# Three inner norms cut into two token halves, interleaved with the matmul units before and behind them

## What is computed

```python
h = modulate(rmsnorm(x, p['norm_mix_g']), mod[0], mod[1])
q, k, v, u_r, u_f = split_projection(h, p['w_in'])
...                                    # attention, RWKV scans, Fourier mixing -> o
x = x + g1 * o                         # o is the output projection
h = modulate(rmsnorm(x, p['norm_ffn_g']), sh2, sc2)
gt, up = jnp.split(h @ p['ffn_w_in'], 2, axis=-1)
return x + g2 * ((jax.nn.silu(gt) * up) @ p['ffn_w_out'])

def rmsnorm(x, g):
    y = x * lax.rsqrt(jnp.mean(x * x, axis=-1, keepdims=True) + RMS_EPS)
    return y * g
def modulate(h, shift, scale):
    return h * (1.0 + scale) + shift
```

## Time and profile before

| | |
|---|---|
| median of three runs | 1829.46 us (1827.52 to 1830.53) |
| span of the profiled execution | 1825.5 us |
| the profiled execution's own time | not given apart from its span; the median lies 3.96 us above the span |
| mean granted clock of TensorE | 0.996 |
| PE busy | 1741.5 us, 95% |
| DVE, ACT, POOL busy | 1064.4, 803.0 and 370.7 us |

### The profile page before, as it was taken

How to read it: one execution, slowest core, us unless ns; L and a number is a source line. 1 busy time by engine, 2 the same in 40 slices (tenths; PEclk the granted TensorE clock), 3 DMA queues, 4 the chain that set the end, 5 groups by cost and what they waited for, 6 DMA issues and landing times. The chain is left out here.

```text
span 1825.5 us, 46192 instructions
## 1 busy us (share of the span) xinstructions
PE 1741.5 (95%) x19693; PEld 1629.2 (89%) x19693; DVE 1064.4 (58%) x2330; ACT 803.0 (44%) x1729; POOL 370.7 (20%) x306
## 2 busy tenths in 40 slices
PE   7999988889999999999999999898999999999997
PEld 5999776779899999999989987777898999999997
DVE  4545777663494673838453566676519647365663
ACT  3343655542453351535443356464326525344352
POOL 3254010212202003020324431002231120201112
PEclk9999999999999999999999999999999999999999
DMA  9654401004513313141327360010122132323211
GB/s 338 211 131 145 120 5 49 6 4 135 168 59 89 85 60 103 58 115 53 99 83 202 97 193 21 17 36 7 29 66 56 63 108 64 105 61 90 84 56 58
DMA packets 215973, 161.11 MB, mean 88 GB/s; under 512 B 21968, under 2 KB 213146, under 8 KB 215770
## 3 DMA queue, kind: packets, MB, share of 16 engines
q1 hardware_dynamic: 213818, 156.13, 29.0%
q0 software_dynamic: 1952, 2.03, 0.4%
HBM read 154.99 MB, written 3.15 MB: 87 GB/s over the span
## 5 line engine op out<-in xcount | busy, mean ns | idle before, releaser
L2683 DVE SCALAR_TENSOR_TENSOR x<-PS,mod,x 128x320 f32<-128x320 f32 (+2 forms) x240 | 90.8, 434 | 289.3 <-PE PS L1082 289.3
L1118 PE MATMUL PS<-T_hi,wsplit 128*128 128x320 f32 x768 | 170.0, 309 | 0.0
L822 POOL TENSOR_TENSOR SfR<-ring,SfR 128x768 fp32r<-128x768 f32 (+1 forms) x24 | 41.1, 1712 | 582.3 <-ACT SfR L1792 582.3
L1081 PE MATMUL PS<-in_hi,win 128*128 128x320 f32 x480 | 149.9, 320 | 0.7 <-POOL win L822 0.7
L1082 PE MATMUL PS<-in_hi,win 128*128 128x320 f32 x480 | 144.6, 309 | 0.0
L1081 PE MATMUL PS<-hid_hi,wsplit 128*128 128x320 f32 x440 | 133.0, 310 | 0.0
L1082 PE MATMUL PS<-hid_hi,wsplit 128*128 128x320 f32 x440 | 132.5, 309 | 0.0
L1118 PEld LDWEIGHTS PS<-T_hi,wsplit 128*128 128x128 f32 x768 | 128.4, 188 | 0.0
L1118 PE MATMUL PS<-h_hi,wsplit 128*128 128x320 f32 x576 | 127.6, 309 | 0.0
L1118 PE MATMUL PS<-T_lo,wsplit 128*128 128x320 f32 x384 | 118.7, 309 | 0.0
L2110 ACT ACTIVATE wsplit<-Sf 128x512 fp32r<-128x512 f32 x96 | 59.8, 629 | 130.0 <-DVE Sf L2733 72.3
(11 more groups left out here) (540 smaller groups left out, 5407.2 us busy)
## 6 DMA issues: line engine op xcount, KB each, us to landing
ring<-in_w_ada SPq DMA_DIRECT2D x47, 1024.0 KB, 6.7
ring<-in_ffn_w_in SPq DMA_DIRECT2D x88, 512.0 KB, 5.2
ring<-in_ffn_w_out SPq DMA_DIRECT2D x16, 768.0 KB, 4.3
ring<-in_ffn_w_out SPq DMA_DIRECT2D x16, 640.0 KB, 4.0
ring<-in_w_in SPq DMA_DIRECT2D x7, 1024.0 KB, 9.5
ring<-in_w_in SPq DMA_DIRECT2D x10, 512.0 KB, 6.0
ring<-in_w_in SPq DMA_DIRECT2D x16, 256.0 KB, 6.0
ring<-in_w_out SPq DMA_DIRECT2D x16, 256.0 KB, 5.8
```

The lines of the kernel that those rows point to most:

```text
L822: nc.gpsimd.tensor_tensor(lo, raw_w, hi, SUB).then_inc(wl_ready(), 1)
L1081: mm(lat[:, 0:TH], w, v[:, 0:TH], start=(n == 0), stop=(n == total - 1))
L1118: last = mm(bank[:, 0:TH], (w_lo if p == 1 else w_hi)[:, k, :], (v_lo if p == 2 else v_hi)[:, k, :], start=(q in (A11, A12, S1_) and k == ...
L2683: last = V.scalar_tensor_tensor(x[:, m, a:b], bank[:, at:at + b - a], mod[:, gate_at + m, s:s + 1], x[:, m, a:b], MUL, ADD)
```

## The change

The two units in front of each inner norm and the two behind it run by token halves, with the norm's steps in between.

- `last_two`: left half of unit 6, `pair_part` of tile 5, left half of unit 7, then (only at A) the modulation matmuls, then the right halves of both, into which the sums (`half_sums`) and the spread (`half_spread`) of the left half are put.
- `first_two`: for each half the products with the high parts of both units, tile by tile, then those with the residues. The sums of the right half stand behind tile 4 of the left half, its spread behind tile 7.
- Scaling on DVE is a plain product of `x` and the spread result (`half_scale`); gain and shift go together on ACT (`half_high`). For residues of tiles 0 to 3 ACT writes `h` in full precision (`half_full`) and POOL subtracts (`low_half`); for tiles 4 to 7 DVE does both (`half_low`).
- The first scale of the left half waits for the whole of unit 7 (`ready(names[1])`). The `warm` matmuls at the inner norms go. Weights of FFN0 and FFN0 + 1 get places of their own and are split earlier. The parameters of layer 1 are turned earlier; two entries leave the list of PSUM items.

```diff
+                def low_half(la, which, half):
+                    hi, lo = (h_hi, h_lo) if which else (in_hi, in_lo)
+                    c = slice(TH * half, TH * half + TH)
+                    for k in range(KP):
+                        e.wait_ge(full_act.sem, full_act.upto(la, KP * (2 * which + half) + k + 1))
+                        nc.gpsimd.tensor_tensor(lo[:, k, c], h[:, k, c], hi[:, k, c], SUB).then_inc(hl_pool(), 1)
...
-                for u in range(FFN0, NUNIT):
+                weight_low(FFN0)
+                weight_low(FFN0 + 1)
+                low_half(l, 1, 0)
+                weight_low(FFN0 + 2)
+                low_half(l, 1, 1)
+                for u in range(FFN0 + 3, NUNIT):
...
+                def half_sums(la, which, half):
+                    e.wait_ge(sq_ready.sem, sq_ready.upto(la, which * (KT + 2) + KT + 2 * half))
+                    for k in (KT - 2, KT - 1):
+                        for c in (2 * half, 2 * half + 1):
...
+                def half_spread(la, which, half):
+                    e.wait_ge(rms_inv.sem, rms_inv.upto(la, 2 * which + half + 1))
...
                 def first_two(u):
-                    on_high = [(k, p) for k in range(KT) for p in (0, 1)]
...
-                    unit(u, on_high, 3 * KT)
-                    unit(u + 1, on_high, 3 * KT)
-                    unit(u, on_low, 3 * KT, len(on_high))
-                    unit(u + 1, on_low, 3 * KT, len(on_high))
+                    for half in range(2):
+                        for k in range(KT):
+                            for v in (u, u + 1):
+                                unit(v, [(k, 0), (k, 1)], 3 * KT, 2 * k, (half,), half == 0)
+                            if half == 0 and k == KP:
+                                half_sums(l, which, 1)
...
+                            half_spread(l, which, 1)
+                        unit(u, on_low, 3 * KT, 2 * KT, (half,))
+                        unit(u + 1, on_low, 3 * KT, 2 * KT, (half,))
+
+                def last_two(u, order, total, cut, la, which, done, between):
+                    unit(u, order, total, 0, (0,)).then_inc(done, 1)
+                    pair_part(which, PAIR_ENDS[-1])
+                    unit(u + 1, order, total, 0, (0,)).then_inc(done, 1)
+                    between()
+                    unit(u, order[:10], total, 0, (1,))
+                    half_sums(la, which, 0)
+                    unit(u, order[10:], total, 10, (1,))
+                    unit(u + 1, order[:cut], total, 0, (1,))
+                    half_spread(la, which, 0)
+                    unit(u + 1, order[cut:], total, cut, (1,))
...
-                for m in range(2, KT):
+                for m in range(2, KT - 2):
...
-                pair_part(1, KT - 1)
-                warm(3)
-                inverse(1)
-                warm(4)
+                last_two(NPROJ + KT - 2, early + late, 3 * KT, 4, l, 1, left_out.sem, next_rows)
...
+                for k in range(KT):
+                    half_high(l, 1, 0, k)
+                    if k == 1:
+                        taken(e, l, ("out", KT - 1))
+                        half_square(l, 1, 1, KT - 1)
+                    if k == KP + 1:
+                        half_root(l, 1, 1)
+                half_full(l, 1, 0)
                 weight_high(FFN0 + 2)
+                act(root_table[:, :], eps[:, 0:1], ACT.Silu)
                 for k in range(KT):
...
+                    half_high(l, 1, 1, k)
+                half_full(l, 1, 1)
...
+            def half_low(l, which, half):
...
+                for k in range(KP, KT):
+                    e.wait_ge(h_ready.sem, h_ready.upto(l, KT * (2 * which + half) + k + 1))
+                    for s, a, b in HALVES[half]:
+                        last = V.tensor_scalar(h[:, k, a:b], h[:, k, a:b], gain[:, which, k, s:s + 1],
+                                               mod[:, 24 * which + k, s:s + 1], MUL, ADD)
+                    own.mark(last)
+                for k in range(KP, KT):
+                    e.wait_ge(dve_own, own.n - KT + 1 + k)
+                    V.tensor_tensor(lo[:, k, c], h[:, k, c], hi[:, k, c], SUB).then_inc(hl_ready(), 1)
...
+                    half_inverse(la, which, 0)
+                    free = [acc_free[ITEM_AT[name] % 2] for name in names]
+                    residual_half(names[0], KT - 2, gate_at, 1, None, 0).then_inc(free[0](), 1)
+                    ready(names[1])
+                    e.wait_ge(inv_ps.sem, inv_ps.upto(la, 2 * which + 1))
+                    half_scale(la, which, 0, 0)
+                    half_scale(la, which, 0, 1)
+                    residual_half(names[1], KT - 1, gate_at, 1, None, 0).then_inc(free[1](), 1)
+                    for k in range(2, KT):
+                        half_scale(la, which, 0, k)
+                    half_inverse(la, which, 1)
+                    half_low(la, which, 0)
```

More of the change, by code:

```diff
@@ L1001, in last_part @@
+                def half_spread(la, which, half):
+                    e.wait_ge(rms_inv.sem, rms_inv.upto(la, 2 * which + half + 1))
+                    r = slice(64 * half, 64 * half + 64)
+                    for i in range(2):
+                        last = mm(ps[6 + half][:, QW * i:QW * i + QW], mats[r, 5 + 2 * half + i, :], rot[r, 0:QW],
+                                  start=True, stop=True)
+                    last.then_inc(acc_ready() if which and half else inv_ps(), 1)
                 def last_part(k):
@@ L1052, in ada_cols, with unit @@
                     last.then_inc(mcol_ps(), 1)
-                def unit(u, order, total, first=0):
+                def unit(u, order, total, first=0, parts=(0, 1), held=False):
                     name, ck, g, nk = UNITS[u]
                     if first == 0:
-                        begin(name)
+                        if not held:
+                            begin(name)
                         e.wait_ge(wl_ready.sem, wl_ready.upto(l, u + 1))
@@ L1757, in _, with half_full @@
+            def half_full(l, which, half):
+                for k in range(KP):
+                    for s, a, b in HALVES[half]:
+                        last = act(h[:, k, a:b], h[:, k, a:b], ACT.Identity,
+                                   bias=mod[:, 24 * which + k, s:s + 1], scale=gain[:, which, k, s:s + 1])
+                    last.then_inc(full_act(), 1)
             for q_ in range(2):
                 e.wait_ge(xT_sb[q_], 5)
+            e.sem_inc(full_act(2 * KP), 2 * KP)
             for l in range(DEPTH):
@@ L2056, in _ @@
                     ada_rows(0, ahead)
-                for k in range(KT):
-                    if 0 < k and k + 2 < KT:
+                for k in range(KT - 2):
+                    if 0 < k:
                         weight_high(NPROJ + k + 2)
-                    elif k == KT - 1:
-                        weight_high(FFN0)
                     taken(e, l, ("out", k))
@@ new lines, in first_scale, with half_inverse @@
+                for k in tiles:
+                    e.wait_ge(h_ready.sem, h_ready.upto(0, 2 * (k + 1)))
+                    for s, (a, b) in enumerate(STREAMS):
+                        last = V.scalar_tensor_tensor(in_lo[:, k, a:b], h[:, k, a:b], mod[:, k, s:s + 1],
+                                                      in_hi[:, k, a:b], ADD, SUB)
+                    last.then_inc(hl_ready(), 1)
+            def half_inverse(l, which, half):
+                r = slice(64 * half, 64 * half + 64)
+                e.wait_ge(root_done.sem, root_done.upto(l, 2 * which + half + 1))
+                V.reciprocal(rot[r, 0:QW], rot[r, 0:QW]).then_inc(rms_inv(), 1)
@@ L2685, in residual, with residual_half @@
                     last.then_inc(free(), 1)
-                for m in range(KT):
+                def residual_half(name, m, gate_at, half, done, n):
+                    i, lat, cx = acc_item(name)
+                    if half:
+                        e.wait_ge(acc_ready.sem, acc_ready.upto(l, i + 1))
+                    else:
+                        e.wait_ge(done, n)
+                    for s, a, b in HALVES[half]:
+                        bank = (lat, cx)[half]
+                        last = V.scalar_tensor_tensor(x[:, m, a:b], bank[:, a - TH * half:b - TH * half],
+                                                      mod[:, gate_at + m, s:s + 1], x[:, m, a:b], MUL, ADD)
+                    return last
@@ new lines, in residual_norm @@
+                def residual_norm(la, which, names, gate_at, left, n0, left_done):
+                    for n, name in enumerate(names):
+                        residual_half(name, KT - 2 + n, gate_at, 0, left, n0 + n + 1).then_inc(left_done, 1)
+                    half_inverse(la, which, 0)
[10 more added lines that the diff above has]
+                    half_low(la, which, 0)
+                    if which:
+                        free, lat, cx = ready(("inv", 1))
+                    else:
+                        e.wait_ge(inv_ps.sem, inv_ps.upto(la, 2))
```

(13 more changed lines are left out.)

341 lines of the change are left out of this document (189 added, 152 removed).

## The result

The changed kernel takes **1860.1 us** (median of four runs, 1855.9 to 1863.1) against 1828.9 (four runs, 1827.5 to 1830.5): ratio 1.0165, 95% interval 1.015 to 1.018, so 1.7% slower. Forecast were 1844.5 us and a range of 1826 to 1852: the direction was right, the time lies above the range, and the loss is twice the 15 us of the sum. The profiled execution ran 1859.0 us, span 1857.1, mean granted clock 0.984 (before 1825.5 and 0.996).

A forecast was written before the change was run, and what follows sets the result against it. PE is busy 95% of the span, so a norm costs what PE loses around it. The three inner norms lose 6.1, 4.0 and 4.9 us, together 15.0, on 1829.5: 1844.5 us, range 1826 to 1852.

The forecast's parts named there:

- Front: Before the third inner norm PE waits from 3.5 to 5.9 us for POOL's squares; unit out 7 is whole at 18.5.
- Turns, left half: In the left residues behind a norm DVE and POOL alternate, one instruction each, so DVE ends at 14.95 us; chance 0.60.
- Rival 1: DVE and POOL do not hinder each other in the residues behind the norms: +2 us, 1831 in all; chance 0.18.
- Rival 2: PE never waits for a residue behind the norms: -14 us together, 1815 in all; chance 0.12.
- ACT does each tile in two pieces (192 and 128 columns), 0.65 a tile.: Right half behind the norm: ACT is slower than PE's 0.59 us a tile, last tile ready at 20.75 us.
- POOL's four turns alternate with DVE's: Right half's residues: POOL and DVE take turns after the rewritten `h`, POOL ending at 26.05 us.
- PEclk 1.00: Expected sign in the profile after: TensorE's clock stays at the 2.4 GHz level.
- rival 3: TensorE's clock falls without `warm` matmuls; right half's high products take 9.4 us, not 4.7, per norm: +29, 1859; chance 0.10.
- Ada chunks: At the first inner norm the modulation matmuls wait 1.4 us for their two 1 MB chunks, issued behind out 7's weight residue.
- At nothing: DVE's sums for the fast products behind the units cost nothing; 1 us at first and third inner norms if cover fails.

The follow-up runs named there:

- e2_early: Changed kernel with the weight split of unit FFN0 + 2 done before the left residues instead of behind them: 1857.4 us, ratio 1.0165.
- e4_dve: Changed kernel with the residues of all eight tiles on DVE in both halves, none on POOL: 1853.3 us, ratio 1.0141.
- e5_piece: Changed kernel with the right half's ACT and DVE scalar instructions in one piece of 320 columns, for timing only: 1851.5 us, ratio 1.0129.
- e1_warm: Changed kernel with matmuls that nobody reads put where PE waits behind the three inner norms: 1851.8 us, ratio 1.0143.
- e6_code: Changed kernel with 24 semaphore increments that nobody waits for in PE's program behind each of the first two inner norms: 1855.7 us, ratio 1.014.
- e10_ada: Changed kernel with the first inner norm's modulation matmuls moved from behind the left half of out 7 to behind its right half: 1857.4 us, ratio 1.0159.
- e11_place: Kernel before with only 24 semaphore increments that nobody waits for added in PE's program behind the first inner norm: 1834.5 us, ratio 1.0036.

## Why the prediction was right or wrong

Right, by its own steps:
- **Front.** PE waits 2.12 us in front of the third sum at C (2.3 forecast), 1.50 at B (1.7), none at A; E is 18.9 us behind the start at C (18.5) and 13.0 at B (12.4).
- **Turns, left half.** The first scale of the right half comes at E + 15.03 at C, E + 14.8 at A and E + 12.6 at B; the sum had 14.95 and, without the weight residue, 12.6. Rival 1 would have had DVE through at 9.7. e2_early and e4_dve show the turns by themselves. That the sum fits to 0.1 us at C is in part luck: DVE starts its part at E + 7.4 and not 6.9, its first two scalar instructions come 0.36 us apart and not 0.22, and the whole part lasts 7.6 us, not 8.0.
- **Rival 2** is out: the waits for residues at C are 0.46, 0.49, 0.66, 2.13, 1.27 and three of 0.41, together 6.2 us, over the 5.6 of its condition, though well under my 10.4.
- **Rival 1's price** has a slip at B: 34.5 against 34.6 is -0.1 and not +0.3. Nothing hangs on it.

Wrong, and the step that failed:
- **"ACT does each tile in two pieces (192 and 128 columns), 0.65 a tile."** It takes 0.84, and 0.85 for each rewritten `h` instead of 0.65. The last high product's tile is ready at E + 22.2 at C, 20.75 forecast; POOL's last residue is done at E + 27.7, 26.05 forecast. This is 1.5 us in each norm, and e5_piece shows that ACT's pace is what the right half waits for. I had interpolated between 512 and 128 columns, 0.71 and 0.39, of an instruction that adds the shift and nothing more. The changed instruction applies the gain too, as its scale, and that has a price of its own. The two forms on 128 columns, grouped by shape (busy us, mean ns), in the changed kernel at its first norm, which is not edited, and at C:

```profile
L1823 ACT ACTIVATE in_hi<-h,mod 128x128 fp32r<-128x128 f32 x8 | 3.1, 385 | 0.0
L1834 ACT ACTIVATE h_hi<-h,mod,gain 128x128 fp32r<-128x128 f32 x8 | 3.9, 481 | 0.0
```

That is 0.1 us an instruction, and 0.19 a tile of two pieces: the whole gap between 0.65 and 0.84. The change moved the gain from DVE to ACT, and the sum took this as free.
- **"POOL's four turns alternate with DVE's"** in the right half, with residues that PE takes 1.2 us apart. They do not: DVE does its four in a row, POOL's first is held for 2.09 us behind them, and PE takes POOL's residues 0.82 us apart. From POOL's first start to its last end it is 4.56 us, where 4.65 were forecast, so the sum does not show the fault; that is luck.
- **"PEclk 1.00", and rival 3 at 0.10.** The clock did fall, as the rival said, and its total of 1859 was met by accident. Its price was not: it put 4.7 us a norm on the right half's high products. They run under ACT's pace, and PE still waits 1.27 us (C) and 2.08 (A) for POOL's first residue behind them, so half clock is free there. Behind B it costs 1.7 us on the last 13 matmuls (e1_warm). Behind A and C these end together with DVE's held sum, so it costs nothing alone. In front of E it costs about 1.5 where it happens to stand (C in e1_warm, e2_early, e4_dve, e5_piece, e6_code and e10_ada). The Trainium skill (TensorE: Matmul & The Clock Gate, What's actually happening) says that an idle array drops to half clock; the trace agrees, with 0.88, 0.88 and 0.90 in the three windows where PE waits and no `warm` matmul stands.
- **Ada chunks.** 2.52 us instead of 1.4 at A; E comes 21.4 us behind the start, 19.9 forecast.
- **"At nothing": the fast products.** I had 1 us if the cover fails. DVE's first sum is held by POOL for 2.2 us more at A and C, and 1.3 us come back later.
- **Not in the sum at all:** 5.1 us in the recurrence of layer 1, which goes with the place of PE's code. The forecast looked only at the three norms and took every stretch that isn't edited as unchanged. e11_place loses as much there without the cut in halves, and e6_code takes the loss out of the changed kernel with the cut in place.

So of 31.6 us, 15.0 were forecast, 9.9 more are in the norms and 5.1 go with the code's place. The 9.9 are: ACT's pace, 1.5 in each; the time to E, 1.5 more at A (1.1 of it the chunks), 0.6 at B and 0.4 at C; the clock behind the last residue at B, 1.7; and at A and C 1.8 to 1.9 which clock and held sum share, less the 1.3 won back. The 1.8 us at the first norm stay open, and layer 0's recurrence gives 0.2 back; the kernel before shows as much there from one execution to another (in e11_place, unedited up to A, its first norm was 3.9 us longer and that recurrence 1.7).

## What to carry to other kernels

Cutting a norm in halves puts more instructions on the engines between two matmul stages (at B 80 for scales, shifts and residues, where 48 stood), and these were the bound: count pieces, not columns, before counting what PE can hide, and price an instruction in the form that it will have, with all its operands. Where two engines hold each other up, splitting one job over both buys next to nothing (0.6 us of 6.1 here), and another instruction of the second engine is paid by the first; look for what stands behind the wait that you remove. One trace of a stretch is one draw: look at a stretch that no edit touches before you credit a repair with a few us. When a change alters the number of instructions of an engine, compare the stretches that it doesn't touch too, and put the same number of idle instructions into the old kernel before blaming the idea.

## What the runs showed of the hardware

ACT: an instruction on 128 columns takes 0.385 us with the shift alone and 0.481 with shift and gain. In the changed kernel one of 128 columns is followed by the next 0.39 us later, one of 192 after 0.44 and one of 320 after 0.55. From these I estimate 0.28 us for the instruction and 0.83 ns for a column.

DVE and POOL: a scalar instruction on 320 columns (e4_dve, eight in 2.94 us) costs 0.36 us alone; the eight beside one POOL instruction of 2.34 us take 4.98.

PE: the traces suggest that its program is loaded while it runs, and that a stretch of small matmuls can run into the end of what is loaded. The profile page of the changed kernel has a queue for instructions (packets, MB, share):

```profile
q8 instruction: 156, 2.56, 0.6%
```

2.56 MB in 156 transfers is 16 KB each. PE's waits for issue of 0.4 us or more in layer 1's recurrence follow them closely: in the changed kernel thirteen of thirteen end 2.2 to 2.9 us behind the start of such a transfer and 1.3 to 1.8 behind its end; in the kernel before five, four of them 2.4 to 2.9 behind a start. The longest of one window of the changed kernel, behind a transfer that ran from 1160.30 to 1161.23:

```profile
1162.56 0.34 PE L1605 MATMUL PS<-mix 64*64 64x128 f32 x4 [1.33 <-issue]
```

The queue's records don't say whose code a transfer brings, so that it is PE's own next 16 KB is inferred from this timing and from e11_place, where 24 instructions moved the waits to other lines. Which numbers of instructions are good was not tried: three kernels (before, e6_code, e1_warm) wait 3.6 to 4.5 us for issue there, the others 5.1 to 9.7. How many of these us are the place and how many one execution's draw is open too, beyond the kernels that e11_place and e6_code compare.
